# Moving the RWKV sample step from a normalisation stage into a chunk stage, on GpSimd, with rows spread through memory

## The reference, cut to what matters

```python
def step(S, inp):
    r_t, k_t, v_t, d_t, kk_t, a_t = inp
    S = (S * d_t[:, :, None, :]
         - jnp.einsum('bhvk,bhk->bhv', S, kk_t)[..., None] * (kk_t * a_t)[:, :, None, :]
         + v_t[..., None] * k_t[:, :, None, :])
    return S, jnp.einsum('bhvk,bhk->bhv', S, r_t)
...
mean = jnp.mean(y, axis=-1, keepdims=True)
var = jnp.mean(jnp.square(y - mean), axis=-1, keepdims=True)
y = ((y - mean) * lax.rsqrt(var + GN_EPS_B)).reshape(bsz, L, D_B) * ln_w + ln_b
y = y + (jnp.sum(r * k * r_k, axis=-1, keepdims=True) * v).reshape(bsz, L, D_B)
return y * g, proj[:, -1], sT
```

## Time and profile before

| | |
|---|---|
| median of three runs | 2339.72 us |
| the profiled execution | 2343.12 us |
| its span, first to last instruction | 2341.3 us |
| mean granted TensorE clock | 0.929 of full |
| TensorE busy | 2105.8 us, 90% |
| VectorE busy | 661.2 us, 28% |
| ScalarE busy | 343.9 us, 15% |
| GpSimd busy | 137.1 us, 6% |

### The profile page before, as it was taken

The page is one execution under the profiler, slowest core; times in us unless marked ns, Lnnn a source line. Parts: engine busy times, 40 slices in busy tenths (PEclk is TensorE's granted clock), DMA queues, the critical chain, the costliest instruction groups (busy, mean ns, idle before and its releaser), DMA issues. The chain is left out here.

```text
span 2341.3 us, 32274 instructions
## 1 busy us (share of the span) xinstructions
PE 2105.8 (90%) x13264; PEld 1857.5 (79%) x13264; DVE 661.2 (28%) x1039; ACT 343.9 (15%) x630; POOL 137.1 (6%) x153
## 2 busy tenths in 40 slices
PE   6988998589999999998998787779999999999577
PEld 5876997378888888876887466669999999999566
DVE  4377565721000000035412754410000000000053
ACT  1553111110000000011131110100111111011011
POOL 0001101412000000001002000010000000000100
PEclk9998999799999999999999668759999999999778
DMA  4211000029222222222222001047887777887510
GB/s 156 63 54 54 2 2 24 18 98 380 76 77 72 85 80 74 72 67 86 72 73 92 41 21 37 1 177 266 281 276 252 255 263 258 279 280 256 192 64 37
DMA packets 74177, 293.38 MB, mean 125 GB/s; under 512 B 8576, under 2 KB 9728, under 8 KB 72816
## 3 DMA queue, kind: packets, MB, share of 16 engines
q1 hardware_dynamic: 63504, 254.95, 32.3%
q0 software_dynamic: 8256, 29.64, 3.4%
q10 hardware_dynamic: 2336, 7.62, 1.0%
HBM read 254.87 MB, written 37.31 MB: 125 GB/s over the span
## 5 line engine op out<-in xcount | busy, mean ns | idle before, releaser
L193 PE MATMUL ps<-normed,ring 128*128 128x260 f32 (+1 forms) x3424 | 766.0, 386 | 16.7 <-DVE normed L236 16.7
L193 PEld LDWEIGHTS ps<-normed,ring 128*128 128x128 f32 (+1 forms) x3424 | 655.4, 192 | 124.2 <-issue 22.4
L2232 PE MATMUL ps<-proj,ring 128*128 128x144 f32 x3168 | 394.2, 288 | 6.5 <-DMA ring<-in_w_moe_gu 6.5
L2232 PEld LDWEIGHTS ps<-proj,ring 128*128 128x128 f32 x3168 | 392.2, 192 | 7.0 <-issue 6.9
L2248 PE MATMUL ps<-wide,ring 128*128 128x144 f32 x1584 | 202.8, 288 | 0.0
L2248 PEld LDWEIGHTS ps<-wide,ring 128*128 128x128 f32 x1584 | 196.0, 190 | 0.9
L193 PE MATMUL ps<-proj,ring 128*128 128x260 f32 x640 | 152.1, 400 | 19.0 <-PEq L935 8.5
L193 PEld LDWEIGHTS ps<-proj,ring 128*128 128x128 f32 x640 | 127.7, 200 | 41.5 <-issue 14.0
L193 PE MATMUL ps<-wide,ring 128*128 128x260 f32 x704 | 154.6, 383 | 0.9 <-DVE wide L1244 0.9
L193 PEld LDWEIGHTS ps<-wide,ring 128*128 128x128 f32 x704 | 134.0, 190 | 21.5 <-DVE wide L1244 1.3
L2296 DVE TENSOR_TENSOR wide<-temps,ps 128x144 f32<-128x144 f32 x99 | 30.2, 305 | 399.6 <-PE ps L2232 399.6
(11 more groups left out here) (458 smaller groups left out, 1756.8 us busy)
## 6 DMA issues: line engine op xcount, KB each, us to landing
ring<-in_w_moe_gu SPq DMA_DIRECT2D x198, 512.0 KB, 4.4
ring<-in_w_moe_dn SPq DMA_DIRECT2D x72, 704.0 KB, 5.7
ring<-in_w_gu SPq DMA_DIRECT2D x44, 512.0 KB, 3.5
ring<-in_w_in_cd SPq DMA_DIRECT2D x25, 512.0 KB, 3.5
ring<-in_w_in_ab SPq DMA_DIRECT2D x22, 512.0 KB, 3.5
ring<-in_w_dn SPq DMA_DIRECT2D x16, 704.0 KB, 4.0
ring<-in_w_ple SPq DMA_DIRECT2D x16, 640.0 KB, 3.9
x_slots<-zeros POOLq DMA_DIRECT2D x19, 512.0 KB, 21.1
```

What stands on the lines that cost most here:

```text
L193: mm = pe.matmul(dst[0:width, a:a + HALF], slab[:, k * width:(k + 1) * width], x[:, a:a + HALF], start=first and k == 0, stop=last and k = ...
L2232: mm = pe.matmul(hid_psum(m, s), slot(Q_MOE + 2 * m + s)[:, f * P:(f + 1) * P], XG[:, f * W:(f + 1) * W], start=f == 0, stop=f == KD - 1)
```

## The change

The samples' step leaves the normalisation stage and runs in the chunk stages, and group norm's root is taken in another layout.

- Spreading: TensorE transposes the five kinds (160 columns of `small`) into PSUM at the start of the chunk block, VectorE copies them into `zeros`, SyncE writes them to a scratch tensor in memory (`smp_rows`), waits, and reads each kind back as one row of 8 KB for 64 partitions at a time (`rows_of`). The ring's slots hold the state and the spread rows meanwhile, so the first output-projection slabs are loaded after the sample state is stored and the second sums are taken, instead of in the input projection.
- Arithmetic: GpSimd does seven multiplies, subtractions and additions of 128x2048 (`sample_sums` ahead of its work for stage 1, `sample_states` ahead of that for stage 2). VectorE does the two row sums, each in four parts of 512 columns, in levels 1 to 4 of stages 0 and 2 (`sample_sum`). The first part waits for GpSimd's product.
- Group norm: the squares' sums are formed token-major (tokens in rows, 32 columns for all heads), by products with the squares as weights; the root and the reciprocal are taken of 128x32; ScalarE widens the result by broadcast (`RWIDE`), TensorE transposes it back by products with the identity, VectorE multiplies from PSUM. The gate is formed early, in other banks. Bias is added to the bonus term by GpSimd ahead; VectorE does weight and sum in one instruction; GpSimd is left with the gate's multiply.
- The samples' state is laid out head pair first, sample second, on the host too (not shown).

The diff, cut to what is added where a block is rewritten (the text before is above; a two-column indent stands for four):

```diff
@@ -139,6 +139,7 @@
...
 x_slots = nc.dram_tensor("x_slots", [(MAXB + 2) * W, D], F32, kind="Internal").ap()
+smp_rows = nc.dram_tensor("smp_rows", [2, 5 * 2048], F32, kind="Internal").ap()
 y_slots = nc.dram_tensor("y_slots", [(MAXB + 2) * W, D], F32, kind="Internal").ap()
@@ -367,8 +368,6 @@
...
-    for q in range(RING):
-      load_slab(sp, Q_OUT0 + q, i["w_out_ab"][q * P:(q + 1) * P, :])
@@ -625,6 +624,8 @@
...
+dg_ready, bc_mm, bc_read, st_in, norm_a, norm_b = map(signal, (
+  "dg_ready", "bc_mm", "bc_read", "st_in", "norm_a", "norm_b"))
 names = ("ab_mm", "al_read", "am_mm", "am_read", "bk_mm", "bk_read", "v_mm", "v_read", "d_ready", "e_mm",
@@ -635,6 +636,21 @@
...
+SR4 = [ring[:, n * 2048:(n + 1) * 2048] for n in range(4)]
+S_ST, S_KK, S_D, S_BB = SR4
+S_K, S_R = S_KK, S_D
+by_row = lambda ap: ap.rearrange("p (r k) -> p r k", k=64)
+row_sum = small[:, 256:288]
+sv_row = smp[:, SV].rearrange("p t b -> p (t b)")
+sm_in = [signal(f"sm_in{n}") for n in range(4)]
+sm_tr, sm_kept, sm_out, sm_prod, sm_sum, sm_state = map(signal, (
+  "sm_tr", "sm_kept", "sm_out", "sm_prod", "sm_sum", "sm_state"))
+sm_fetched, sm_used = signal("sm_fetched"), signal("sm_used")
+def spread_row(ap):
+  return ap.unsqueeze(2).broadcast_to([P, 32, 64])
@@ -652,6 +668,32 @@
...
     loaded.on(sp.dma_start(Dm[:, 0:961], i["ph_rw"]), 16)
+    st_in.on(sp.dma_start(S_ST, i["s_rw"]), 16)
+    def rows_of(kind, dst, done):
+      for hh in range(2):
+        src = smp_rows[hh, 2048 * kind:2048 * kind + 2048].unsqueeze(0).broadcast_to([64, 2048])
+        done.on(sp.dma_start(dst[64 * hh:64 * hh + 64, :], src), 16)
+    sp.wait_ge(sm_kept.sem, sm_kept.at(1))
+    for n, w_ in ((0, P), (P, 32)):
+      dst = smp_rows.rearrange("h (r k) -> r h k", k=64)[n:n + w_]
+      src = zeros[0:w_, n:n + P].rearrange("r (h k) -> r h k", h=2)
+      sm_out.on(sp.dma_start(dst, src), 16)
+    sp.wait_ge(sm_out.sem, sm_out.count)
+    rows_of(SKK, S_KK, st_in)
+    rows_of(SD, S_D, sm_in[0])
+    rows_of(SBB, S_BB, sm_in[1])
+    sp.wait_ge(sm_sum.sem, sm_sum.at(1))
+    rows_of(SK, S_K, sm_in[2])
+    sp.wait_ge(sm_used.sem, sm_used.at(1))
+    rows_of(SR, S_R, sm_in[3])
+    sp.wait_ge(sm_state.sem, sm_state.at(1))
+    stored.on(sp.dma_start(o["wkv_s"], S_ST), 16)
+    sp.wait_ge(sm_sum.sem, sm_sum.at(2))
+    sp.wait_ge(stored.sem, stored.count)
+    for q in range(RING):
+      load_slab(sp, Q_OUT0 + q, i["w_out_ab"][q * P:(q + 1) * P, :])
@@ -661,7 +703,29 @@
...
+    def sample_sums():
+      pool.wait_ge(st_in.sem, st_in.count)
+      S(pool.tensor_tensor(S_KK, S_ST, S_KK, ALU.mult), sm_prod)
+      pool.wait_ge(sm_in[0].sem, sm_in[0].count)
+      S(pool.tensor_tensor(S_ST, S_ST, S_D, ALU.mult), sm_used)
+    def sample_states():
+      pool.wait_ge(sm_in[1].sem, sm_in[1].count)
+      pool.wait_ge(sm_sum.sem, sm_sum.at(1))
+      S(pool.tensor_tensor(by_row(S_BB), by_row(S_BB), spread_row(row_sum), ALU.mult))
+      S(pool.tensor_tensor(S_ST, S_ST, S_BB, ALU.subtract))
+      pool.wait_ge(sm_in[2].sem, sm_in[2].count)
+      S(pool.tensor_tensor(by_row(S_K), by_row(S_K), spread_row(sv_row), ALU.mult))
+      S(pool.tensor_tensor(S_ST, S_ST, S_K, ALU.add), sm_state)
+      pool.wait_ge(sm_in[3].sem, sm_in[3].count)
+      S(pool.tensor_tensor(S_R, S_ST, S_R, ALU.mult), sm_prod)
     for s in range(1, 4):
+      if s == 1:
+        sample_sums()
+      elif s == 2:
+        sample_states()
       w(pool, "al_read", s + 1)
@@ -709,9 +773,13 @@
...
+    for n, w_ in ((0, P), (P, 32)):
+      mm = pe.transpose(ps[0][0:w_, n:n + P], small[:, 32 + n:32 + n + w_], ident)
+    sm_tr.on(mm)
     products_ab(0)
...
       products_am(0, cc)
+    pe.wait_ge(sm_kept.sem, sm_kept.at(1))
     token_major(0, BK_HOME(0), RB, "bk_mm")
@@ -875,6 +943,18 @@
...
+    def sample_sum(n, part):
+      src = by_row((S_KK, S_R)[n])[:, 8 * part:8 * part + 8]
+      if part == 0:
+        dve.wait_ge(sm_prod.sem, sm_prod.at(n + 1))
+        if n:
+          dve.wait_ge(sm_state.sem, sm_state.at(1))
+      S(dve.tensor_reduce(row_sum[:, 8 * part:8 * part + 8], src, AX.X, ALU.add), sm_sum if part == 3 else None)
+    dve.wait_ge(sm_tr.sem, sm_tr.at(1))
+    S(dve.tensor_copy(zeros[:, 0:P], ps[0][:, 0:P]))
+    S(dve.tensor_copy(zeros[0:32, P:2 * P], ps[0][0:32, P:2 * P]), sm_kept)
     dve.wait_ge(loaded.sem, loaded.count)
@@ -883,6 +963,8 @@
...
       for l in range(5):
+        if s in (0, 2) and l:
+          sample_sum(s // 2, l - 1)
         masked_g(s, l, 0)
@@ -910,179 +992,110 @@
...
+scaled, rstd_ready, rstd_wide, rstd_mm = map(signal, ("scaled", "rstd_ready", "rstd_wide", "rstd_mm"))
+RWIDE = lambda t: B[:, 6144 + t * SEQ:6144 + (t + 1) * SEQ]
 gn_bank = lambda t: ps[2 + t // 2][:, 512 * (t % 2):512 * (t % 2) + SEQ]
+G_BANKS = (1, 2, 3, 1)
+g_bank = lambda t: ps[G_BANKS[t] // 2][:, 512 * (G_BANKS[t] % 2):512 * (G_BANKS[t] % 2) + SEQ]
+var32, sm_mean, sm_g, sm_var = ps[0][:, 0:32], ps[1][:, 0:32], ps[1][:, 32:64], ps[1][:, 512:544]
+RSTD = small[:, 300:332]
 sqr = lambda t: xr(8 + t)[:, 0:SEQ]
...
+ysm, ysq = row_sum, Dm[:, 2592:2624]
 tb_ = lambda ap: ap.rearrange("p (t b) -> p t b", t=4)
...
+    for t in range(4):
       mean_mm.on(pe.matmul(gn_bank(t), blk, yr[:, t, 0:SEQ], start=True, stop=True))
...
+    for t in range(4):
+      if t == 3:
+        pe.wait_ge(g_read.sem, g_read.at(1))
+      g_mm.on(pe.matmul(g_bank(t), g2[:, t * P:(t + 1) * P], xr(13)[:, 0:SEQ], start=True, stop=True))
+    for t in range(4):
       pe.wait_ge(sq_ready.sem, sq_ready.at(t + 1))
...
+      for c in range(4):
+        mm = pe.matmul(var32[:, 8 * t + 2 * c:8 * t + 2 * c + 2], sqr(t)[:, c * P:(c + 1) * P], blk[:, 0:P:64],
+               start=True, stop=True)
+    var_mm.on(mm)
+    pe.wait_ge(g_read.sem, g_read.at(2))
+    pe.matmul(sm_mean, blk, ysm, start=True, stop=True)
     for t in range(4):
...
+      mm = pe.matmul(sm_g[:, 8 * t:8 * t + 8], g2[:, t * P:(t + 1) * P], xr(13)[:, SEQ:T], start=True, stop=True)
+    mean_mm.on(mm)
     for t in range(4):
...
+      pe.wait_ge(rstd_wide.sem, rstd_wide.at(t + 1))
+      for c in range(4):
+        mm = pe.matmul(gn_bank(t)[:, c * P:(c + 1) * P], RWIDE(t)[:, c * P:(c + 1) * P], ident, start=True, stop=True)
+      rstd_mm.on(mm)
+    pe.wait_ge(g_read.sem, g_read.at(3))
     pe.wait_ge(sq_ready.sem, sq_ready.at(5))
...
+    var_mm.on(pe.matmul(sm_var, blk, ysq, start=True, stop=True))
...
       sq_ready.on(act.activation(sqr(t), yr[:, t, 0:SEQ], ACT.Square))
+      act.wait_ge(g_mm.sem, g_mm.at(t + 1))
+      g_read.on(act.activation(gb(t), g_bank(t), ACT.Copy))
+    act.wait_ge(var_mm.sem, var_mm.at(1))
+    root_ready.on(act.activation(RSTD, var32, ACT.Sqrt, bias=small[:, 1:2], scale=1.0 / 64))
+    act.wait_ge(rstd_ready.sem, rstd_ready.at(1))
     for t in range(4):
...
+      rstd_wide.on(act.activation(RWIDE(t).rearrange("p (n k) -> p n k", k=64),
+                    RSTD[:, 8 * t:8 * t + 8].unsqueeze(2).broadcast_to([P, 8, 64]), ACT.Copy))
     act.wait_ge(cent.sem, cent.at(5))
...
+    act.wait_ge(var_mm.sem, var_mm.at(2))
+    root_ready.on(act.activation(ysq, sm_var, ACT.Sqrt, bias=small[:, 1:2], scale=1.0 / 64))
...
+      xk = xr(4 + t)[:, 0:SEQ]
+      S(pool.tensor_scalar(xk, xk, v("ln_b", t), None, ALU.add))
+    for t in range(4):
       pool.wait_ge(scaled.sem, scaled.at(t + 1))
...
+      pool_step.on(pool.tensor_tensor(yr[:, t, 0:SEQ], yr[:, t, 0:SEQ], gb(t), ALU.mult))
...
+    for t in range(4):
       dve.wait_ge(mean_mm.sem, mean_mm.at(t + 1))
...
+    S(dve.scalar_tensor_tensor(out=ysm, in0=sm_mean, scalar=-1.0 / 64, in1=ysm, op0=ALU.mult, op1=ALU.add), cent)
+    dve.wait_ge(root_ready.sem, root_ready.at(1))
+    S(dve.reciprocal(RSTD, RSTD), rstd_ready)
+    for t in range(4):
+      y = yr[:, t, 0:SEQ]
+      dve.wait_ge(rstd_mm.sem, rstd_mm.at(t + 1))
+      S(dve.tensor_tensor(y, y, gn_bank(t), ALU.mult))
+      dve.wait_ge(pool_step.sem, pool_step.at(t + 1))
+      S(dve.scalar_tensor_tensor(out=y, in0=y, scalar=v("ln_w", t), in1=xr(4 + t)[:, 0:SEQ],
+                   op0=ALU.mult, op1=ALU.add), scaled)
+    dve.wait_ge(root_ready.sem, root_ready.at(2))
     S(dve.reciprocal(ysq, ysq))
...
+    S(dve.tensor_tensor(yr[:, :, SEQ:T], tb_(ysm), tb_(sm_g), ALU.mult))
 end_of_block()
@@ -2483,7 +2496,7 @@
...
-  a["s_rw"] = x["state_rwkv_wkv"][0].reshape(NS, 4, 2 * 64, 64).transpose(2, 0, 1, 3).reshape(P, 2048)
+  a["s_rw"] = x["state_rwkv_wkv"][0].reshape(NS, 4, 2 * 64, 64).transpose(2, 1, 0, 3).reshape(P, 2048)
   flat = lambda y: y.reshape(-1, y.shape[-1])
@@ -2524,7 +2537,7 @@
...
-  wkv_s = r["wkv_s"].reshape(2, 64, NS, 4, 64).transpose(2, 3, 0, 1, 4).reshape(NS, 8, 64, 64)
+  wkv_s = r["wkv_s"].reshape(2, 64, 4, NS, 64).transpose(3, 2, 0, 1, 4).reshape(NS, 8, 64, 64)
   c2 = r["cd_small"]
```

More of the change, by code:

```diff
@@ L946, in _ @@
             def _(pe):
-                def broadcast(n):
-                    pe.wait_ge(dg_ready.sem, dg_ready.at(n + 1))
-                    if n:
```

(72 more changed lines are left out.)

42 lines of the change are left out of this document (removed).

## The result

The kernel after takes 2305.11 us (median of four runs, 2301.43 to 2308.6), the kernel before, run beside it, 2340.11 (2336.74 to 2341.12): a ratio of 0.9852, 95% interval 0.9841 to 0.9864, and 35.0 us less. The profiled execution took 2305.02 us. Of the kernel of experiment 2, two of four executions ran at a mean granted clock of 0.727 and 0.553 (2848.66 and 3682.72 us), and are left out of its time.

What follows compares the result with a forecast made beforehand. VectorE, ending the normalisation stage, was taken as the bound: 64.5 us becoming 27.0 gains 37.5, less 0.5 in the chunk stages, 37.0; median 2339.7 becomes 2303. Forecast spread 2297 to 2308, range 2294 to 2314.

Steps and rivals of the forecast that it cites:

- sample tail ends: End of normalisation stage: one reciprocal, one multiply blocked until 23.95, six more operations at 0.35, ending at 26.4 us.
- What bounds the stage: Normalisation stage: VectorE ends it; without the sample work and wide reciprocals a new chain takes 27.0 us instead of 64.5.
- rival 4: Normalisation stage: sample work does not set its end, a 35 us centring-to-root chain remains; gain 29, 2311 us; chance 0.06.
- Clock kept: Normalisation stage: TensorE, busy without a gap from 0.0 to 12.5 us, stays at full clock; sums 1.0 us per tile.
- rival 1: Normalisation stage: clock lost, small products for sums, samples and transposes at half speed; +6.7 us, 2309 us; chance 0.12.
- a sign of being wrong: Normalisation stage: half clock in the transposing products, which were charged 1.0 us per tile, would show the prediction wrong.
- The wait between VectorE and GpSimd: Normalisation stage: VectorE's scale-and-add waits for GpSimd's gate multiply, 1.9 us per tile; 1.4 without the wait.
- Chunk stages: Chunk stages: GpSimd's added work stays hidden; VectorE's partial reductions cost 0.5 us over two stages.
- cover: Chunk stage 0: GpSimd's first product ready at 238.5, wanted by VectorE at 244.05, 5.5 us of cover.
- the first trip through memory: Start of chunk stages: write lands within 5.1 us, by 228.5; first kind of rows takes 5.2 us, to 233.7.
- GpSimd's load: Chunk stages: seven GpSimd operations of 128x2048, two at 3.8 and five at 4.7, 31.1 us; decay's wait 0.4, costing nothing.
- Rival 3: Chunk stages: slow 64-fold row reads; at 22.8 us per kind the gain is gone, at 25, 2351 us; chance 0.03.

Runs made afterwards that it cites:

- experiment 2: Kernel after, with the 16 products of the squares' sums moving 128 columns instead of 2: 2302.19 and 2302.92 us.
- Experiment 1: Kernel after, with sums of squares, root and reciprocal again at full width (128x512 per tile), the sample move kept: 2310.01 us, ratio 0.9869.
- experiment 7: Kernel after, with gate products behind the sums and root, and the squares' sums' products 128 columns wide: 2296.22 us, ratio 0.9812.
- Experiment 5: Kernel after, with GpSimd's four gate multiplies waiting for VectorE's last scale-and-add: 2305.19 us, ratio 0.9855.
- experiment 4: Kernel after, with the first-wanted kind of spread rows read third instead of first: 2314.96 us, ratio 0.9883.
- Experiment 6: Kernel after, with four more GpSimd operations of 128x2048 in the chunk stages, results unused: 2305.5 us, ratio 0.9854.

## Why the prediction was right, step by step

The forecast was 2303, inside its own spread of 2297 to 2308; 2305.1 came. Measured from the first mean, as there:

| step | predicted | measured |
|---|---|---|
| sums of squares end | 11.2 | 11.7 |
| sample products end | 12.5 | 13.9 |
| reciprocal ends | 13.45 | 14.6 |
| first multiply from PSUM starts | 15.25 | 17.5 |
| tile 3 leaves VectorE | 22.6 | 24.7 |
| GpSimd ends | 23.95 | 26.0 |
| sample tail ends | 26.4 | 27.8 |
| first output product | 27.0 | 28.35 |

- **What bounds the stage: right.** Experiment 1 shows the root on the chain with 6.8, and 29.4 for the move with the rest of the rewrite; rival 4, a long chain without the samples' work, is out, since the stage takes 28.35.
- **Clock kept: wrong, 2.2 us.** The prediction held against rival 1 that TensorE is busy without a gap. It was, and the clock fell nevertheless. The sums took 4.79 instead of 4.0, the small sample products 2.3 instead of 1.3 and the transposes began at half speed (5.79 for the four tiles instead of 4), which the prediction had named as a sign of being wrong. Rival 1 came true in a third of its price of 6.7: the clock fell only in the course of the sums, which lost 0.8 instead of 4.0, and behind the first tile VectorE and GpSimd set the pace, not the transposes. Experiments 2 and 7 show which products bring it. Some luck was in the sum: with the clock kept through the sums (experiment 2) the reciprocal ends at 12.37, 1.1 sooner than forecast, and the first multiply, behind transposes at 0.55, starts at 15.27 for 15.25. The terms ahead of the root were thus charged too high by about what the clock takes behind it.
- **The wait between VectorE and GpSimd: right.** 1.9 us per tile was charged, and the last scale-and-adds start 1.89 apart; tiles and tail together took 0.9 less than summed, most of it in the tail, which was charged by upper bounds. Experiment 5 shows that GpSimd makes the wait: the scale-and-adds take 0.75 without it and up to 1.13 with it. The Trainium skill's rule on the shared port pair (SBUF — State Buffer, "SBUF: two separate sides") agrees.
- **Chunk stages: right that the work hides, by a thinner cover.** That 0.41 came for 0.5 is luck, since the chunk stages scatter by 1.1 between profiles. The product was ready 3.1 later after the start of the stage than reckoned: the first read was issued 1.1 later, the first kind of rows took 7.45 in place of 5.2, less 0.3 on GpSimd (4.53 for 4.7 and a hand-over). Of 5.5 us cover 2.2 were left; experiment 4 shows what the next microseconds would have cost. The term that was mis-sized is the first trip through memory, which was priced by the transfers of the earlier trace rows. Why it took longer is not shown: the rows repeat, but the plain load of the state took 7.2 for 5.2 as well. The output weights' loads were six, from 344.62, not three; TensorE did not wait for them.
- **GpSimd's load: right.** 4.53 and 3.62 per operation against 4.7 and 3.8; the decay kept its 0.42, though it ran from 275.05 to 275.47 across the end of GpSimd's third multiply (275.18) and the start of its add. By 0.26 us more of overlap, in experiment 4, it took 0.67: that it met nothing was close. Experiment 6 adds four operations at no cost that the runs show.
- **Rival 3, slow rows: out.** A kind of rows takes 4.8 to 5.4 us once the reads run, far from the 22.8 at which the change would have paid nothing.

Of the 37.0 us forecast, the two stages gave 36.14 - 0.41 = 35.7; the medians moved by 35.0.

## What to carry to other kernels

Work moved off a chain into a stage with an idle engine is worth the chain's length, not the work's; reckon the chain anew, and reckon the cover of the first transfer in the new place most carefully: here it was the term that shrank most, from 5.5 us to 2.2. When a chain of products is reworked into narrow ones, read the granted clock of the new stretch before durations from elsewhere are trusted: here products with 64 times the columns took less time. When two engines hold each other up, as VectorE and GpSimd did here, shifting the one's work may only move the wait to what the other does next (experiment 5); put it beside an operation that is not lengthened, as the 128x512 reciprocal was not in experiment 1.
